# Norms summed on TensorE, three chunks at a layer's start, and weight sums on VectorE in a two-layer float32 encoder

## The chip, the cores and the metric

The kernel runs on one core of a Trainium2 chip. The metric is device time in microseconds (us), from the start of the program to its end, with the host left out. Engines are called PE (TensorE), DVE (VectorE), ACT (ScalarE), POOL (GpSimd) and SP (the queue that issues most transfers).

## The reference

Two batches of 512 tokens (b = 0 and b = 1), width 1024, go through two layers with shared weights, all in float32:

```python
def trunk(x, ...):
    for i in range(2):
        h = rms_norm(x, norm_mix[i])               # x * rsqrt(mean(x*x) + 1e-6) * g
        x = x + (pool_mixer(h, ...) if i == 0 else attention_mixer(h, ...))
        h = rms_norm(x, norm_ffn[i])
        x = x + swiglu_ffn(h, w_gate_up[i], w_down[i])

def swiglu_ffn(h, w_gate_up, w_down):
    gu = h @ w_gate_up                             # 1024 -> 2 x 2816
    g, u = gu[..., :2816], gu[..., 2816:]
    return (silu(g) * u) @ w_down                  # 2816 -> 1024
```

The pool mixer takes centred window means over 2, 4, 8 and 16 tokens minus the token, and multiplies each quarter of the width by a 256 x 256 matrix. The attention has 8 query heads and 2 key heads of 128, with a norm and a rotation on queries and keys.

## The kernel before

**Layout.** x lies transposed: features on partitions, x[:, c, token] with 8 feature chunks c of 128, tokens 0 to 511 for b = 0 and 512 to 1023 for b = 1. A float32 product is made from two fp32r parts of each factor (hi, a cast on ACT; lo, a subtraction on DVE), as three matmuls: hi*hi, hi*lo, lo*hi (`three`).

**Gate and up.** The 2816 hidden features are 22 chunks i of 128. Both batches and both halves of the width are combined in a scheme of seven products instead of eight (`gate_up(layer, i, k)`, k = 1 to 7): the moving tiles are B11 and B21 (b = 0), B22, and the combinations T1 to T4 of both batches; the stationary ones are quarters of the weights (A11, A12, A22) and their sums S1 to S4. One product is 12 matmuls of 128x512. This text writes (i, k) for product k of chunk i: (0, 5) is the first that needs T1, so the first that needs the norm of b = 1. k = 5, 6 and 7 need S1, S2, S3, and k = 3 needs S4. The four sums of a chunk are made of its raw weights: by POOL for chunks 0 and 1 of each layer (`block_sums_13`, `block_sums_24`), by DVE for the others (`block_sums`). POOL also makes the 4 tiles of T3 and the 4 of T4 (`t3_full`, `t4_full`). Each weight part is then cast and subtracted into `ring` (`w_split`). PSUM banks 0 to 2 serve even chunks, 3 to 5 odd ones (`g_bank`), and two sets of four tiles hold their results (`act_tiles`, `snap_*`).

**Down.** Seven products again (q = 0 to 6), of 6 blocks each: 42 blocks, of 24 matmuls, or 12 for a product's last. Block k needs weights `wd` (A11 for q = 0, A12 for q = 1, then sums made in `down_sum`) and activations that come back from memory (`load_act`). SP issues both, in program order; after `load_act(k)` for k = 3 and up come two weight loads each. `load_act(k)` waits until block k - 2 is split. `down_sum(0)` stands on DVE behind `block_lo(3)`, and waits for the first two blocks of A21, which share a semaphore.

**Norms.** Three of them (k = 1: before layer 0's gate/up; 2: before attention; 3: before layer 1's gate/up), for each batch: ACT squares 8 chunks (`square`), POOL adds them one after the other (`add_squares`), PE multiplies the sum by a matrix of ones, so that all partitions hold the sum (`mean_square`), ACT takes the root, DVE the reciprocal of 128x512 (`inverse`), and then DVE scales x (`b0_full`, `b1_full`, `norm_full`).

Every engine's order is written out by hand; semaphores tie them, and an instruction that waits holds up all behind it on its engine.

## Time and profile before

| | us |
|---|---|
| three runs | 1827.1, 1822.15, 1824.36 (median 1824.36) |
| the profiled execution | 1823.22 |
| its span | 1821.4 |
| outside its span | 1.8 |

The granted TensorE clock is 0.976 of full speed over the span. The kernel reads 137.23 MB and writes 44.56 MB, 100 GB/s over the span. A timeline row gives the start, the duration, the engine, line and operation, what is written and read, how many instructions the row merges, and in brackets how long the engine was idle before it and what ended that. A matmul's recorded duration has its latency in it: in a dense stretch one starts each 0.227 us, whatever the row says a single one took. A float32 matmul, not fp32r, is recorded as two.

### The profile page before, as it was taken

How to read it: one execution, taken by the hardware profiler on the slowest of the kernel's cores; microseconds unless marked ns; L12 is line 12 of the kernel's file. 1: busy time of each engine (PE TensorE's matmuls, PEld its weight loads, DVE VectorE, ACT ScalarE, POOL GpSimd, SP SyncE). 2: the span in 40 equal slices, each digit the busy share in tenths (PEclk: the TensorE clock that was granted, in tenths of full speed). 3: DMA queues.
4: the chain of work that ended last, by engine and by line, in shares of the span. 5: the costliest groups of instructions: out<-in, count | busy, mean ns of one | idle time of the engine just before them, and what ended most of it. 6: DMA issues, size and time to landing. Idle time of an engine off the chain costs nothing. (4 is left out here: it accounts for less than half of the span.)

```text
span 1821.4 us, 20998 instructions
## 1 busy us (share of the span) xinstructions
PE 1717.3 (94%) x7741; PEld 1409.0 (77%) x7741; DVE 1205.1 (66%) x1620; ACT 760.7 (42%) x1149; POOL 202.0 (11%) x155
## 2 busy tenths in 40 slices
PE   6779999999999999899998999799999999989998
PEld 6657888888877888778776787578888888878887
DVE  5786656666547756756878877876566665557744
ACT  6543333333333335434576554343333333333332
POOL 1430000000000003322124212500000000000000
PEclk9889999999999999999999999899999999999999
DMA  4003423224275332143112112023233232473333
GB/s 170 24 12 121 129 90 113 93 93 133 76 270 197 101 94 90 58 133 103 42 54 63 35 47 81 24 93 116 87 109 117 93 116 87 156 289 116 95 98 120
DMA packets 185786, 188.40 MB, mean 103 GB/s; under 512 B 8355, under 2 KB 138453, under 8 KB 185685
## 3 DMA queue, kind: packets, MB, share of 16 engines
q1 hardware_dynamic: 112884, 150.36, 25.5%
q10 hardware_dynamic: 72800, 36.70, 6.9%
q8 instruction: 62, 1.02, 0.2%
q14 instruction: 40, 0.32, 0.1%
HBM read 137.23 MB, written 44.56 MB: 100 GB/s over the span
## 5 line engine op out<-in xcount | busy, mean ns | idle before, releaser
L664 PE MATMUL bank<-h_T,ring 128*128 128x512 f32 x2112 | 508.9, 393 | 20.0 <-DVE h_T L1512 11.2
L664 PEld LDWEIGHTS bank<-h_T,ring 128*128 128x128 f32 x2112 | 399.8, 190 | 108.6 <-issue 10.8
L689 PE MATMUL bank<-a,w 128*128 128x512 f32 x1848 | 426.1, 393 | 10.9 <-DVE a L1638 10.9
L689 PEld LDWEIGHTS bank<-a,w 128*128 128x128 f32 x1848 | 349.8, 190 | 85.8 <-issue 12.9
L664 PE MATMUL bank<-h_B,ring 128*128 128x512 f32 x1584 | 388.9, 395 | 9.9 <-ACT tmp L1037 4.3
L664 PEld LDWEIGHTS bank<-h_B,ring 128*128 128x128 f32 x1584 | 300.6, 190 | 78.4 <-ACT tmp L1037 5.2
L1565 DVE TENSOR_TENSOR ring<-raw,ring 128x512 fp32r<-128x512 f32 (+1 forms) x178 | 147.7, 831 | 48.3 <-ACT ring L1016 48.1
L1016 ACT CAST ring<-raw 128x512 fp32r<-128x512 f32 (+1 forms) x178 | 128.5, 722 | 69.7 <-PE bank L664 53.7
L1090 ACT CAST w<-wd_A 128x1024 fp32r<-128x1024 f32 x72 | 70.6, 981 | 199.8 <-PE bank L689 199.8
L1634 DVE TENSOR_TENSOR w<-wd_A,w 128x1024 fp32r<-128x1024 f32 x72 | 82.6, 1147 | 97.3 <-ACT w L1090 97.2
L2112 POOL TENSOR_TENSOR tmp<-tmp,tmp 128x512 f32<-128x512 f32 x42 | 62.5, 1488 | 749.8 <-ACT tmp L938 747.5
L546 PE MATMUL bank<-half_hi,aw 128*128 128x512 f32 x320 | 111.9, 408 | 4.6 <-DVE aw L1459 3.9
L1577 DVE TENSOR_TENSOR tmp<-bank,tmp 128x512 f32<-128x512 f32 x44 | 30.4, 691 | 124.9 <-PE bank L664 124.6
L1638 DVE TENSOR_TENSOR a<-raw,a 128x1024 fp32r<-128x1024 f32 x84 | 97.0, 1154 | 6.5 <-ACT a L1092 6.5
L1092 ACT CAST a<-raw 128x1024 fp32r<-128x1024 f32 x84 | 82.0, 977 | 13.1 <-DMA raw<-act_d 13.1
L546 PE MATMUL bank<-o_hi,aw 128*128 128x512 f32 x256 | 85.6, 397 | 1.5 <-DVE x L1979 1.5
L1016 ACT CAST ring<-s_tmp 128x1024 fp32r<-128x1024 f32 (+1 forms) x46 | 46.7, 1015 | 91.2 <-PE bank L664 85.2
L1343 ACT ACTIVATE prob<-bank,nmax,q_inv 128x512 f32<-128x512 f32 x64 | 49.9, 780 | 70.7 <-DVE nmax L1956 70.7
L546 PEld LDWEIGHTS bank<-half_hi,aw 128*128 128x128 f32 x320 | 61.4, 192 | 19.5 <-issue 3.7
L1053 ACT ACTIVATE tmp<-tmp 128x512 f32<-128x512 f32 x44 | 27.8, 631 | 103.0 <-DVE tmp L1583 103.0
L1565 DVE TENSOR_TENSOR ring<-s_tmp,ring 128x1024 fp32r<-128x1024 f32 (+1 forms) x46 | 54.1, 1177 | 20.7 <-ACT ring L1016 20.7
L1459 DVE TENSOR_TENSOR aw<-raw,aw 128x1024 fp32r<-128x1024 f32 x40 | 54.7, 1369 | 16.6 <-ACT aw L925 16.1
(168 smaller groups left out, 2097.9 us busy)
## 6 DMA issues: line engine op xcount, KB each, us to landing
act_d<-tmp SPq DMA_DIRECT2D x154, 256.0 KB, 3.0
raw<-in_ffn_w_gate_up ACTq DMA_DIRECT2D x70, 512.0 KB, 3.9
raw<-act_d SPq DMA_DIRECT2D x70, 512.0 KB, 3.5
wd_A<-in_ffn_w_down SPq DMA_DIRECT2D x40, 512.0 KB, 6.7
raw<-in_attn_w_qkv SPq DMA_DIRECT2D x24, 512.0 KB, 3.9
raw<-in_ffn_w_gate_up SPq DMA_DIRECT2D x18, 512.0 KB, 4.2
raw<-in_attn_w_o SPq DMA_DIRECT2D x16, 512.0 KB, 4.2
tmp<-tmp SPq DMA_DIRECT2D x80, 64.0 KB, 2.0
```

The source lines that it names most:

```text
L546: ins = pe.matmul(out, w, m, start=first and i == 0, stop=last and i == n - 1)
L664: ins = pe.matmul(out[:, :], w, m, start=k in (1, 2, 5) and j == 0 and t == 0, stop=k in (2, 3, 4) and j == 3 and t == 2, skip_group_check ...
L689: ins = pe.matmul(banks[m][:, :], w, h, start=q in (0, 1, 3) and first and t == 0, stop=q in (1, 5, 6) and jj == NBLK - 1 and t == 2, skip ...
L1016: nc.scalar.copy(dst, src).then_inc(f_hi, 1)
L1090: nc.scalar.copy(w2[:, k % 3, 0:n, 0, :], src).then_inc(w2_hi, 1)
L1092: nc.scalar.copy(a2[:, (k + 1) % 3, 0:n, 0, :], raw2[:, act_slot(layer, k), 0:n, :]).then_inc(a2_hi, 1)
L1343: nc.scalar.activation(prob[:, i, :], b_score[s % 2][:, :], ACT.Exp, bias=nmax[:, s % 8:s % 8 + 1], scale=q_inv[:, s:s + 1], accum_out=rsu ...
L1459: nc.vector.tensor_tensor(aw[:, slot(i), 1, :], raw[:, i % RAW, :], aw[:, slot(i), 0, :].bitcast(F32), ALU.subtract).then_inc(w_lo, 1)
L1565: nc.vector.tensor_tensor(lo, src, hi.bitcast(F32), ALU.subtract).then_inc(f_lo, 1)
L1634: nc.vector.tensor_tensor(w2[:, k % 3, 0:n, 1, :], src, w2[:, k % 3, 0:n, 0, :].bitcast(F32), ALU.subtract).then_inc(w2_lo, 1)
L1638: nc.vector.tensor_tensor(a2[:, s, 0:n, 1, :], raw2[:, act_slot(layer, k), 0:n, :], a2[:, s, 0:n, 0, :].bitcast(F32), ALU.subtract).then_i ...
L2112: nc.gpsimd.tensor_tensor(out=stat[b][:, :], in0=stat[b][:, :], in1=sqr[i % 2][:, :], op=ALU.add).then_inc(n_acc, 1)
```

## The change

- **Norms.** PE sums the squares. A tile of squares is the stationary side and a column of ones the moving one, four small matmuls to a tile (`columns`, `sum_square`), added up in one PSUM bank. This gives the sum of each token in a column, so root and reciprocal work on 128x4. DVE multiplies the identity by it (a diagonal), PE multiplies ones by the diagonal, which spreads it over all partitions (`wide`), and ACT copies that to `stat` (`keep_wide`). For k = 1 all 16 tiles are summed so, for k = 2 the last 4, for k = 3 the last; POOL adds up the others as before, and PE takes that sum in by columns too.
- **Start of a layer's gate/up.** Chunk 2 gets banks 6, 7 and 2, so that (1, 1), (1, 2), (2, 1) run ahead of (0, 5). The tiles of results are seven instead of eight: silu of g0 goes where g1's was, and T4 goes into a tile of the even chunk.
- **Weight sums.** DVE makes all block sums, and T3 and T4; POOL none.
- **Down loads.** A12's first two blocks are loaded ahead of the last stores, and A21 and A22 in pairs.

```diff
+        DIRECT = {1: SEQ[1], 2: SEQ[2][12:], 3: SEQ[3][15:]}
-        g_bank = [bank[0:3], bank[3:6]]
+        g_bank = [bank[0:3], bank[3:6], [bank[6], bank[7], bank[2]]]
...
+            def columns(src, out, first):
+                for i in range(NT):
+                    ins = pe.matmul(out[:, i:i + 1], src[:, i * P:(i + 1) * P], ones[:, 0:1],
+                                    start=first and i == 0, stop=True, skip_group_check=True)
+                return ins
+            def wide(k, b, out):
+                pe.wait_ge(n_diag, 2 * (k - 1) + b + 1)
+                pe.matmul(out[:, :], ones[:, :], diag[k][:, :], start=True, stop=True).then_inc(n_wide, 1)
...
             def square(k, r, ready):
+                    if i - ADD0[k] > len(sq_ring[k]):
+                        act.wait_ge(n_add, i - len(sq_ring[k]))
...
             def inverse(k, b):
+                cols = n_inv[:, NT * b:NT * (b + 1)]
                 dve.wait_ge(n_sqrt, 2 * (k - 1) + b + 1)
-                nc.vector.reciprocal(stat[b][:, :], stat[b][:, :]).then_inc(n_rstd, 1)
+                nc.vector.reciprocal(cols, cols).then_inc(n_rstd, 1)
+                nc.vector.tensor_tensor(diag[k][:, :].rearrange("p (i t) -> p i t", i=NT),
+                                        ident[:, :].unsqueeze(1).to_broadcast([P, NT, P]),
+                                        cols.unsqueeze(2).to_broadcast([P, NT, P]), ALU.mult).then_inc(n_diag, 1)
...
+            for c in range(4):
+                sum_square(1, c, bank[3])
+            turn_x(1, range(4))
+            for c in range(4, KC):
+                sum_square(1, c, bank[3])
+            turn_x(1, range(4, KC))
+            wide(1, 0, bank[3])
+            pool(1, 3)
...
             def swiglu(layer):                     # PE
                 gate_up(layer, 0, 1)
-                mean_square(k, 1, bank[7])
+                if layer == 0:
+                    sum_square(1, 14, bank[3])
+                else:
+                    mean_square(3, 1, bank[3])
+                sum_square(k, 15, bank[3])
                 gate_up(layer, 0, 2)
+                wide(k, 1, bank[5])
                 gate_up(layer, 1, 1)
+                gate_up(layer, 1, 2)
+                gate_up(layer, 2, 1)
                 gate_up(layer, 0, 5)
-                gate_up(layer, 1, 2)
+                gate_up(layer, 2, 2)
                 gate_up(layer, 1, 5)
...
                 for b in range(N_BLOCK):
                     if layer == 0 and b == N_BLOCK - NBLK + 2:
-                        mean_square(2, 0, bank[1])
+                        mean_square(2, 0, bank[1]).then_inc(n_ms, 1)
+                    elif layer == 0 and b == N_BLOCK - NBLK + 4:
+                        wide(2, 0, bank[1])
...
-            project(0, b_gate[0], 0)
-            mean_square(2, 1, b_down[3])
-            project(1, b_gate[1], 0)
+            for quarter in range(3):
+                project(0, b_gate[0], 0, quarter)
+            mean_square(2, 1, b_up[1])
+            for r in range(12, 16):
+                sum_square(2, r, b_up[1])
+            project(0, b_gate[0], 0, 3)
+            project(1, b_gate[1], 0, 0)
+            project(1, b_gate[1], 0, 1)
+            wide(2, 1, b_up[1])
+            project(1, b_gate[1], 0, 2)
+            project(1, b_gate[1], 0, 3)
...
              for w in range(7, 16):
                 project_out(w)
-                if w == 9:
-                    mean_square(3, 0, bank[1])
+                if w == 8:
+                    mean_square(3, 0, bank[1]).then_inc(n_ms, 1)
+                elif w == 9:
+                    wide(3, 0, bank[1])
...
+            def t4_full(layer, j):                 # DVE, was POOL's
+            def t3_full(layer, j):
...
                 later = []
-                for jj in range(NBLK):
-                    if jj < 3:
-                        later += [("A12", 2 * jj), ("A12", 2 * jj + 1)]
-                    later += [("A21", jj), ("A22", jj)]
+                for jj in range(0, NBLK, 2):
+                    later += [("A21", jj), ("A21", jj + 1), ("A22", jj), ("A22", jj + 1)]
+                    if jj < 4:
+                        later += [("A12", jj + 2), ("A12", jj + 3)]
```

How the order moves, at three places. First PE, where layer 0's gate/up begins. h0_B11, h0_B21, h0_T1 and h0_T2 are the moving tiles; a row with h0 is one product, and its bank tells the chunk (0 to 2: chunk 0; 3 to 5: chunk 1). Before:

```order
L664 MATMUL bank0<-h0_B11_80,ring_98 128x512 x12
L559 MATMUL bank7<-tmp7_77,ones_121 128x512
L664 MATMUL bank1<-h0_B21_81,ring_98 128x512 x12
L664 MATMUL bank3<-h0_B11_80,ring_98 128x512 x12
L664 MATMUL bank2<-h0_T1_86,ring_98 128x512 x12
L664 MATMUL bank4<-h0_B21_81,ring_98 128x512 x12
L664 MATMUL bank5<-h0_T1_86,ring_98 128x512 x12
L664 MATMUL bank0<-h0_T2_82,ring_98 128x512 x12
```

And now (banks 6 and 7 are chunk 2's):

```order
L725 MATMUL bank0<-h0_B11_80,ring_98 128x512 x12
L577 MATMUL bank3<-ones_121,tmp2_72 128x1 x4
L577 MATMUL bank3<-ones_121,tmp1_71 128x1 x4
L725 MATMUL bank1<-h0_B21_81,ring_98 128x512 x12
L598 MATMUL bank5<-tmp3_73,ones_121 128x512
L725 MATMUL bank3<-h0_B11_80,ring_98 128x512 x12
L725 MATMUL bank4<-h0_B21_81,ring_98 128x512 x12
L725 MATMUL bank6<-h0_B11_80,ring_98 128x512 x12
L725 MATMUL bank2<-h0_T1_86,ring_98 128x512 x12
L725 MATMUL bank7<-h0_B21_81,ring_98 128x512 x12
L725 MATMUL bank5<-h0_T1_86,ring_98 128x512 x12
L725 MATMUL bank0<-h0_T2_82,ring_98 128x512 x12
```

Between the norm's matmul (L559, now L598) and the first product on T1 stands one product before, and three now; one more, (2, 2), stands before (1, 5).

Second PE again, in the last product of layer 0's down, where the norm for the attention is made. A block is eight rows like those with a2 (four for the last). Before, ahead of block 38, then now, at the end of block 39 and the start of block 40:

```order
L689 MATMUL bank5<-a2_107,w2_106 128x512 x3
L559 MATMUL bank1<-tmp6_76,ones_121 128x512
L689 MATMUL bank6<-a2_107,w2_106 128x512 x3
L689 MATMUL bank7<-a2_107,w2_106 128x512 x3
L689 MATMUL bank4<-a2_107,w2_106 128x512 x3
```

```order
L750 MATMUL bank4<-a2_107,w2_106 128x512 x3
L750 MATMUL bank5<-a2_107,w2_106 128x512 x3
L598 MATMUL bank1<-tmp1_71,ones_121 128x512
L750 MATMUL bank6<-a2_107,w2_106 128x512 x3
L750 MATMUL bank7<-a2_107,w2_106 128x512 x3
```

The column sums (L577) stand where L559 stood, and the matmul that spreads the result stands two blocks later.

Third SP, from the last down load of A11 on (raw2 is the tile of `load_act`; the rows that write act_d are stores). Before:

```order
L388 DMA wd_A11_100<-in_ffn_w_down 128x512
L352 DMA act_d<-tmp5_75 128x512
...
L407 DMA raw2_108<-act_d 128x1024
L388 DMA wd_A12_101<-in_ffn_w_down 128x2x512 x2
L407 DMA raw2_108<-act_d 128x1024
L388 DMA wd_A21_102<-in_ffn_w_down 128x2x512
L388 DMA wd_A22_103<-in_ffn_w_down 128x2x512
L407 DMA raw2_108<-act_d 128x512
L388 DMA wd_A12_101<-in_ffn_w_down 128x2x512 x2
L407 DMA raw2_108<-act_d 128x1024
L388 DMA wd_A21_102<-in_ffn_w_down 128x2x512
```

And now:

```order
L405 DMA wd_A11_100<-in_ffn_w_down 128x512
L405 DMA wd_A12_101<-in_ffn_w_down 128x2x512 x2
L369 DMA act_d<-tmp5_75 128x512
...
L424 DMA raw2_108<-act_d 128x1024
L405 DMA wd_A21_102<-in_ffn_w_down 128x2x512 x2
L424 DMA raw2_108<-act_d 128x1024
L405 DMA wd_A22_103<-in_ffn_w_down 128x2x512 x2
L424 DMA raw2_108<-act_d 128x512
L405 DMA wd_A12_101<-in_ffn_w_down 128x2x512 x2
```

The first rows of raw2 in both are `load_act(3)`. The second load of A21 stood behind `load_act(6)`; it stands behind `load_act(3)` now.

## Rows read from the trace of the kernel before

**Rows 1.** Page, part 1: busy us, share of the span, instructions.

```profile
PE 1717.3 (94%) x7741; PEld 1409.0 (77%) x7741; DVE 1205.1 (66%) x1620; ACT 760.7 (42%) x1149; POOL 202.0 (11%) x155
```

**Rows 2.** Waits of PE: total us, times, longest us.

```profile
PE bank L559 <- POOL tmp L2112: 14.0, 4, 8.5
PE bank L689 <- DVE a L1638: 10.9, 4, 4.8
```

**Rows 3.** Timeline of PE, layer 0's first norm, b = 0.

```profile
47.58 2.07 PE L559 MATMUL bank<-tmp,ones 128*128 128x512 f32 x2 [3.18 <-POOL tmp L2112]
...
56.50 0.47 PE L546 MATMUL bank<-half_hi,pw_hi 128*128 128x512 f32 x1 [0.48 <-ACT x L1111]
```

**Rows 4.** Timeline of PE, layer 0's gate/up, chunks 0 to 2.

```profile
71.59 2.88 PE L664 MATMUL bank<-h_B,ring 128*128 128x512 f32 x12
...
84.08 7.71 PE L664 MATMUL bank<-h_B,ring 128*128 128x512 f32 x24
...
108.58 4.40 PE L664 MATMUL bank<-h_T,ring 128*128 128x512 f32 x18 [2.11 <-DVE ring L1565]
...
158.22 2.88 PE L664 MATMUL bank<-h_T,ring 128*128 128x512 f32 x12
```

**Rows 5.** Timeline of PE, layer 1's start of gate/up, chunks 0 to 2.

```profile
1116.79 0.47 PE L546 MATMUL bank<-o_hi,aw 128*128 128x512 f32 x1 [1.54 <-DVE x L1979]
...
1144.08 2.88 PE L664 MATMUL bank<-h_B,ring 128*128 128x512 f32 x12
...
1162.53 1.62 PE L664 MATMUL bank<-h_T,ring 128*128 128x512 f32 x3 [5.80 <-DVE h_T L1512]
...
1175.12 6.68 PE L664 MATMUL bank<-h_T,ring 128*128 128x512 f32 x21 [2.84 <-DVE ring L1565]
...
1223.68 2.88 PE L664 MATMUL bank<-h_B,ring 128*128 128x512 f32 x12
1226.40 2.88 PE L664 MATMUL bank<-h_T,ring 128*128 128x512 f32 x12
```

**Rows 6.** Timeline of DVE, the same stretch.

```profile
1153.54 3.35 DVE L1465 RECIPROCAL tmp<-tmp 128x512 f32<-128x512 f32 x1
...
1182.94 5.75 DVE L1531 TENSOR_TENSOR h_B<-f_t,h_B 128x512 fp32r<-128x512 f32 x4
...
1189.22 2.48 DVE L1537 TENSOR_TENSOR h_T<-f_t,h_T 128x512 fp32r<-128x512 f32 x4
```

**Rows 7.** Timeline of PE, layer 0's down and layer 1's, block 4 first in each.

```profile
549.96 50.34 PE L689 MATMUL bank<-a,w 128*128 128x512 f32 x210 [4.62 <-DVE a L1638]
...
1618.90 21.27 PE L689 MATMUL bank<-a,w 128*128 128x512 f32 x83 [4.82 <-DVE a L1638]
```

**Rows 8.** Timeline of DVE, layer 1's down, `down_sum(0)`.

```profile
1615.26 1.22 DVE L1652 TENSOR_TENSOR wd_A<-wd_A,wd_A 128x1024 f32<-128x1024 f32 x1 [10.46 <-DMA wd_A<-in_ffn_w_down]
```

**Rows 9.** Windows of PE: stretch, us, busy (count), granted clock, DMA share, GB/s.

```profile
549.00:552.00 3.00, 2.04 (x5) 0.50 0.35 78
```

**Rows 10.** Timeline of PE around layer 0's end of down.

```profile
721.17 1.11 PE L559 MATMUL bank<-tmp,ones 128*128 128x512 f32 x2
721.71 19.65 PE L689 MATMUL bank<-a,w 128*128 128x512 f32 x84
742.97 0.50 PE L546 MATMUL bank<-half_hi,aw 128*128 128x512 f32 x1 [1.61 <-DVE aw L1459]
```

**Rows 11.** Timeline of DVE, first scaling by the attention's norm, b = 0 and b = 1.

```profile
728.79 1.41 DVE L1474 SCALAR_TENSOR_TENSOR tmp<-x,vec,tmp 128x512 f32<-128x512 f32 x2
...
757.39 1.42 DVE L1474 SCALAR_TENSOR_TENSOR tmp<-x,vec,tmp 128x512 f32<-128x512 f32 x2
```

**Rows 12.** Timeline: a reciprocal of 128x4; then four column matmuls among dense ones.

```profile
12.23 0.18 DVE L1684 RECIPROCAL tok_rms<-tok_rms 128x4 f32<-128x4 f32 x1 [12.23 <-ACT tok_rms L1106]
...
794.17 0.95 PE L781 MATMUL bank<-ones,tmp 128*128 128x1 f32 x8
794.98 0.48 PE L546 MATMUL bank<-half_hi,aw 128*128 128x512 f32 x1
```

More of the change, by code:

```diff
@@ L436, in load_ffn @@
                     load_wd(layer, "A11", jj)
+                for jj in range(2):
+                    load_wd(layer, "A12", jj)
                 store_act1(layer, NF - 1)
@@ L554, in w_chunk, with sum_square, turn_x @@
                 return aw[:, slot(i), 0, k * P:(k + 1) * P], aw[:, slot(i), 1, k * P:(k + 1) * P]
-            def mean_square(k, b, out):
-                pe.wait_ge(n_acc, 14 * (k - 1) + acc_count(k, last_of(k, b)))
-                pe.matmul(out[:, :], ones[:, :], stat[b][:, :], start=True, stop=True).then_inc(n_ms, 1)
-            pe.wait_ge(ident_made, 2)
-            def turn_x(b):
-                for i in range(NT):
-                    pe.wait_ge(x_in[NT * b + i], 16)
-                for c in range(KC):
+            def columns(src, out, first):
[3 more added lines that the diff above has]
+                return ins
+            def sum_square(k, r, out):
+                c, b = SEQ[k][r]
+                pe.wait_ge(n_sq, 16 * (k - 1) + r + 1)
+                if k == 1 and r == KC:
+                    pe.wait_ge(n_stat, 1)
+                ins = columns(sq_tile(k, r), out, k == 1 and c == 0)
+                ins.then_inc(n_add, 1)
+            def mean_square(k, b, out):
+                pe.wait_ge(n_acc, acc_count(k, last_of(k, b)))
+                return columns(stat[b], out, True)
+            def wide(k, b, out):
+                pe.wait_ge(n_diag, 2 * (k - 1) + b + 1)
+                pe.matmul(out[:, :], ones[:, :], diag[k][:, :], start=True, stop=True).then_inc(n_wide, 1)
+            pe.wait_ge(ident_made, 2)
+            def turn_x(b, chunks):
+                if chunks[0] == 0:
+                    for i in range(NT):
+                        pe.wait_ge(x_in[NT * b + i], 16)
+                for c in chunks:
                     q = KC * b + c
@@ L616, in mix @@
                     product(b_down[q % 4][:, :], parts, True, True, m_filled)
[L618 removed]
+            turn_x(0, range(KC))
             pe.wait_ge(band_landed, 16)
[L620 to L634 removed]
+            for c in range(4):
+                pool(0, c)
+            mix(0, 0)
+            pool(0, 4)
+            pool(0, 5)
+            mix(0, 1)
+            pool(0, 6)
+            pool(0, 7)
+            mix(0, 2)
+            mix(0, 3)
+            for c in range(3):
+                pool(1, c)
+            for c in range(4):
+                sum_square(1, c, bank[3])
[5 more added lines that the diff above has]
+            pool(1, 3)
+            mix(1, 0)
+            pool(1, 4)
+            pool(1, 5)
+            mix(1, 1)
+            sum_square(1, 8, bank[3])
+            sum_square(1, 9, bank[3])
+            pool(1, 6)
+            pool(1, 7)
+            mix(1, 2)
+            sum_square(1, 10, bank[3])
+            sum_square(1, 11, bank[3])
+            mix(1, 3)
+            sum_square(1, 12, bank[3])
+            sum_square(1, 13, bank[3])
             def gate_up(layer, i, k):
@@ L1310, in _ @@
                 square(2, r, x_ffn0)
+            root(2, 1, b_up[1])
             gain(0, b_gate[0])
             split_next(0)
-            root(2, 1, b_down[3])
-            for c in range(4):
+            keep_wide(2, 1, b_up[1])
+            for c in range(2):
                 norm_hi(1, c)
@@ L1318, in _ @@
             split_next(1)
-            for c in range(4, KC):
+            for c in range(2, KC):
                 norm_hi(1, c)
@@ L1802, in swiglu @@
                 t2_full(layer, 2)
+                t4_full(layer, 2)
                 t2_lo(layer, 1)
@@ L1805, in swiglu @@
                 t2_full(layer, 3)
+                t4_full(layer, 3)
                 t2_lo(layer, 2)
-                add_c11(layer, 1)
                 t2_lo(layer, 3)
+                add_c11(layer, 2)
                 for j in range(4):
                     b22_lo(layer, j)
+                for j in range(4):
+                    t3_full(layer, j)
                 w_split(layer, 1, G_S2)
@@ L1859, in swiglu @@
                     block_lo(layer, k)
-                    if 3 <= k < 27:
-                        down_sum(layer, k - 3)
+                    if 4 <= k < 28:
+                        down_sum(layer, k - 4)
                     if k > 6 and k % 6 == 1:
@@ L1865, in _ @@
             swiglu(0)
-            for k in range(38, 41):
-                block_lo(0, k)
+            block_lo(0, 38)
+            block_lo(0, 39)
             inverse(2, 0)
+            block_lo(0, 40)
             norm_full(0, 0)
```

382 lines of the change are left out of this document (194 added, 188 removed).

## The prediction

> **What bounds the kernel now.** First the page: PE is busy for 1717.3 us of the span, DVE for 1205.1 [rows 1]. PE is the bound, and only its idle stretches, its slow ones and its added work matter. Then PE's waits: two releasers stand out, POOL's sums of squares, 14.0 us, and DVE's split of activations in the down part, 10.9 us [rows 2]. Then PE's timeline, to find where the rest is lost. A product starts 2.72 us after the one before in a dense stretch (1223.68 to 1226.40) [rows 5]. So the 21 products of chunks 0 to 2 need 57.1 us. Layer 0 takes from 71.59 to 160.94 (158.22 + 2.72) for them, 89.4 us [rows 4]; layer 1 from 1144.08 to 1229.12, 85.0 us [rows 5]. So 32 and 28 us are lost in the two starts, part of it waiting on DVE. DVE's timeline in that stretch shows a reciprocal of 3.35 us, and operations that take 1.44 us beside POOL (5.75 for four) and 0.62 without it (2.48 for four) [rows 6]. Each down part loses one wait, 4.62 and 4.82 us [rows 7], and DVE then sat 10.46 us on a weight load [rows 8]. After such a wait the granted clock is 0.50, the 1.2 GHz level, at 549 to 552 us [rows 9]: PE was idle for 4.62 us before. The 210 matmuls behind it take 50.34 us, where 210 x 0.227 + 0.16 is 47.8: the slow clock costs 2.5 us more [rows 7].
>
> **Prices.** A reciprocal of 128x4 is 0.18 us [rows 12]; with the diagonal's multiplication (a DVE operation of 128x512, 0.62) and a dependence of 0.1, `inverse` falls from 3.35 to 0.9 us. Four column matmuls hold PE for 0.81 (794.17 to 794.98) to 0.95 us [rows 12]; I take 0.9. There are 21 tiles summed so and 4 sums of POOL taken in so: 25 x 0.9 = 22.5 us more for PE, of which only what fell into waits is free. `wide` is the same matmul as the old one, about 1.0 us, 6 of them as before. The Trainium skill (TensorE: Matmul & The Clock Gate, section "Wait — 56ns, not 53.3ns?") lets a matmul with few columns start about 25 ns after the last; by that the eight recorded parts would take 0.2 us, the 25 groups 5 us, and the forecast would be 17 us lower, as an estimate from that page. The rows 12 do not show that: the stationary side has to be loaded each time. I go by the row.
>
> **Layer 0's pool stage and start: -2.5 us.** Before, PE waits 3.18 us for POOL's sum and reaches `mix(1, 0)` at 56.50 [rows 3]. Now at 44.4 (47.58 less the wait) come four column sums (3.6), 16 of 32 transposes, four sums (3.6), 16 transposes: 57.4. (The 32 transposes take 5.8: they and `pool(1, 3)` lie between 49.6 and 56.0 [rows 3].) Root and `inverse` run beside the last of these; `wide` 1.0 and `pool(1, 3)` 0.9 lead to `mix(1, 0)` at 59.3, 2.8 late. From there the old kernel took 15.1 us to (0, 1); now six sums are added, 5.4, and each pair stands behind a square that waits for DVE's addition of the mixer's result, since it is placed right after the product that feeds it: about 1.5, 1.3 and 0.5 us. (0, 1) starts at 82.6, against 71.59. But the old kernel then waited for POOL and started (0, 2) at 84.08, 24 matmuls in 7.71 us for 5.6 [rows 4]; the new one starts it at 87.2, after two more sums. `wide` ends at 90.9. By the walk below, (2, 4) ends 65.4 us later, 156.5, against 160.94: -4.4. I keep -2.5, since small matmuls and waits may leave the clock low in this stage. Bounds: -7 and +5.
>
> **Layer 1's start: -9.5 us.** The walk, by rows 5 and 6. The norm of b = 0 is ready some 2.4 us earlier (its reciprocal is that much shorter), so the wait of 1.54 goes, and 0.9 of column sums comes: (0, 1) at 1143.4. Two sums, (0, 2) after its weights: 1151.3. DVE first makes chunk 0's four sums and splits behind them, then `inverse`; `wide` ends at 1153.1. Then (1, 1), (1, 2), (2, 1), with 0.7 for a split, and (0, 5), (2, 2): 1167.7. The old wait of 5.80 before (0, 5) is gone: T1 is ready at 1162.5, when PE comes to it at 1162.2. Next comes (1, 5), which needs S1 of chunk 1. DVE has 28 operations from `wide` to that split (6 scalings of b = 1, 10 tiles of T1, T2 and T4 made or split with their lo parts, 3 additions and 4 block sums among them); at 0.66 us, the mean of 0.62 and 0.70 for those that depend on the last, 18.6 us: 1171.7. So PE waits 4.1 there; the old start of (1, 5) was 1175.12. The clock falls again, 2.5. 14 products follow, 38.1 us, with waits of 1.5 for S2 of chunk 1 (19 DVE operations against three products), 1.0 for g1 of chunk 1 and 1.5 for that of chunk 2 (nothing stands between (i, 7) and (i, 4) there now), and 1.7 for chunk 2's sums: 1171.8 + 38.1 + 2.5 + 5.7 = 1218.1, against 1229.12: -11.0. 1.5 for one more fall of the clock: -9.5. Bounds -13 and -3. DVE's eight moved block sums and tiles (16 operations to a layer, with the four of chunk 0, 9.9 us at 0.62) are inside this: they are paid by POOL's stretching of others (0.82 an operation) and two short reciprocals.
>
> **Down: -7.2 and -7.3 us.** `down_sum(0)` stands behind one block more, and its load is issued three blocks of activations earlier. DVE was free for block 4 at 1604.8 (1615.26 - 10.46) and needs two operations of 1.22 for it [rows 8]: 1607.2; PE comes to it at 1614.1 (1618.90 - 4.82) [rows 7]. What is late next is the load for block 6, behind two blocks of cover. So 4.62 + 2.5 and 4.82 + 2.5 us go. Bounds: all, or nothing.
>
> **The norm before the attention: +8 us.** Here the change costs. The old matmul at 721.17 led to the first scaling at 728.79 [rows 10, 11]. Now the column sums stand there, and `wide` behind blocks 38 and 39: 721.17 + 0.9 + 2 x 5.44 = 732.95. With 1.0 for itself and 0.7 for ACT's copy, DVE scales at 734.7, 5.9 later. From there to PE's first projection it took 14.2 us (742.97 - 728.79), DVE without a gap; so PE starts at 748.9 and idles 6.6 us where it idled 1.61. For b = 1 the old path from there to the next scaling was 14.4 us (757.39 - 742.97). The new one has three quarters of a projection (24 matmuls in all; 4.1), five sums (4.5), a quarter (1.4), half a projection (2.7), `wide` and copy (1.7), and about 2 for the clock: 16.4, so the scaling comes 8 us late. The waits behind it (DVE's chain into the keys) move with it, while PE comes 10 us late, so some of the old waits shrink. +8, bounds +5 and +12. Dense PE work follows, and nothing gives it back.
>
> **Sum.** -2.5 - 7.2 + 8.0 - 9.5 - 7.3 = -18.5. Against the profiled execution's 1823.22 us this is 1804.7; the median shown is 1.1 above it: 1806.
>
> **Rivals.**
> - *The early work gains nothing (1818 us).* The column matmuls keep PE at 1.2 GHz in both starts and the new gaps add falls. For it: after 4.62 us of idle the clock is 0.50 [rows 9]. Against: the sums before (0, 1) in layer 1 stand in dense work. Layer 0's start is then +7, layer 1's -7: 12 more than forecast.
> - *The attention's norm is free (1798 us).* The +8 would not show if the old chain had slack. Against: PE waited 1.61 on it at 742.97 [rows 10], so there was none.
> - *The down wait only moves (1820 us).* The same bytes queue on the same 16 DMA engines; another load, A12's or block 6's activations, is late instead. For it: the wait of 10.46 us on a transfer of 512 KB [rows 8] shows a queue. Then 14.5 us stay.
> - *DVE pays (slower, 1832 us).* The 32 operations moved to DVE in the two starts go at the 1.44 us of rows 6 and not at 0.62, in the stretch where DVE is what PE waits for: 32 x 0.82 = 26 us. It decides from 0.56 us an operation over 0.62. Against: 1.44 is seen only where POOL runs, and POOL has nothing left there.
>
> **Numbers.** Below, a measurement of this kernel can tell 0.3% from no change, 5.5 us. Chances: the forecast 0.62 (its own range 1799 to 1813), early work gains nothing 0.14, norm free 0.08, down wait moves 0.09, DVE pays 0.07. Faster is below 1818.9: 0.62 + 0.08 + 0.08 of the 0.14 + 0.03 of the 0.09 = 0.81. Slower is above 1829.8: 0.07. The same: 0.12. The range is 1796 to 1820.
>
> **What would show it.** In the new trace: no wait of PE over 1 us at block 4; `wide` of the attention's norm near 733 and PE's gap of 6 to 7 us before the first projection; (0, 1) of layer 0 near 82 and not 72; PE's largest wait in each start before (1, 5), on DVE; RECIPROCAL of 128x512 only for the keys; column sums at 0.9 us. Wrong would be a wait at (0, 5) of several us, DVE operations at 1.4 us in the starts, or the first projection at 743.

## The result, and the profile after

The changed kernel takes 1808.9 us, the median of its first five runs (1807.7 to 1820.1), a ratio of 0.9926 to the kernel before, 95% interval 0.990 to 0.9952. Six more runs on another chip gave 1810.5 us, ratio 0.9928 (0.9901 to 0.9954). The forecast was 1806 us, range 1796 to 1820, with a chance of 0.81 for faster. Faster is what it is, by 14 to 15 us.

Two executions were profiled. The first had a span of 1818.3 us; the second, of the same kernel, 1805.1. Where they part is the lesson of this case, so both are shown. By the granted clock that each of the eleven runs records, they stand for two kinds: the six of 1806.2 to 1808.9 us have 0.984 or 0.985, the three of 1816.3 to 1822.7 us have 0.975 to 0.979, and the two between have 0.982. Waits of PE in the second (total us, times, longest), against [rows 2]:

```profile
PE bank L725 <- DVE ring L1690: 17.3, 9, 4.6
PE bank L564 <- DVE aw L1564: 10.5, 2, 6.6
PE bank L750 <- DVE a L1767: 1.7, 2, 1.3
```

POOL releases PE only once more, for 0.2 us, the down part's wait is 1.7 us in all where it was 10.9 [rows 2], and the two waits of 4.6 and 6.6 us are the ones the prediction named: before (1, 5) and before the attention's first projection.

Timeline of PE, second execution, layer 0 from the norm to chunk 2 (start, us, engine, line, operation, shape, count, idle before and releaser), against [rows 3, 4]:

```profile
43.66 3.63 PE L577 MATMUL bank<-ones,tmp 128*128 128x1 f32 x32
47.15 1.95 PE L619 MATMUL bank<-ident,xin 128*128 128x128 f32 x16
48.93 3.79 PE L577 MATMUL bank<-ones,tmp 128*128 128x1 f32 x32
...
109.21 7.83 PE L725 MATMUL bank<-h_T,ring 128*128 128x512 f32 x24 [4.54 <-DVE ring L1690]
...
153.70 3.06 PE L725 MATMUL bank<-h_T,ring 128*128 128x512 f32 x12 [0.79 <-DVE tmp L1708]
```

The same in the first execution:

```profile
42.41 3.63 PE L577 MATMUL bank<-ones,tmp 128*128 128x1 f32 x32
45.90 2.80 PE L619 MATMUL bank<-ident,xin 128*128 128x128 f32 x16
48.49 6.83 PE L577 MATMUL bank<-ones,tmp 128*128 128x1 f32 x32
...
160.22 3.04 PE L725 MATMUL bank<-h_T,ring 128*128 128x512 f32 x12 [0.78 <-DVE tmp L1708]
```

The four column sums that take 3.79 us in one take 6.83 in the other, with PE idle in neither, and the last row of this start stands at 153.70 or at 160.22. The granted clock tells why: 1.00 is 2.4 GHz, 0.50 is 1.2 GHz. Windows of PE (stretch, us, busy (count), granted clock, DMA share, GB/s), first execution:

```profile
47.00:50.00 3.00, 3.00 (x16) 0.50 0.01 3
50.00:53.00 3.00, 3.00 (x15) 0.50 0.01 3
53.00:56.00 3.00, 3.00 (x15) 0.50 0.00 0
56.00:59.00 3.00, 3.00 (x15) 0.50 0.00 0
...
86.00:89.00 3.00, 3.00 (x9) 0.50 0.00 0
```

Second execution:

```profile
47.00:50.00 3.00, 3.00 (x30) 1.00 0.03 8
50.00:53.00 3.00, 3.00 (x25) 0.88 0.01 3
53.00:56.00 3.00, 3.00 (x17) 0.55 0.00 0
56.00:59.00 3.00, 3.00 (x17) 1.00 0.00 0
```

From 47 to 50 us 16 matmuls start in the first, at 1.2 GHz, and 30 in the second, although PE is recorded busy for the whole of each window. The first has a second fall around 86 us, behind a wait of 1.40 us for a square: there (0, 1), the first product of the gate/up, takes 5.47 us instead of 3.02. Of the 6.5 us between the two ends of this start, the stretch up to `mix(1, 0)` makes 3.7 and that product with its neighbours 2.7.

Around the end of layer 0's down, second execution, against [rows 10]:

```profile
518.93 46.26 PE L750 MATMUL bank<-a,w 128*128 128x512 f32 x203 [0.42 <-DVE a L1767]
...
709.42 1.04 PE L577 MATMUL bank<-ones,tmp 128*128 128x1 f32 x8
...
721.33 1.02 PE L598 MATMUL bank<-tmp,ones 128*128 128x512 f32 x2
...
737.18 0.79 PE L564 MATMUL bank<-half_hi,aw 128*128 128x512 f32 x1 [6.63 <-DVE aw L1564]
743.54 4.52 PE L577 MATMUL bank<-ones,tmp 128*128 128x1 f32 x40
```

The group of down matmuls is cut at the edge of the view, at 565 us. It runs past the place where block 4 used to wait, and dense: 46.26 us is 203 x 0.227 and the last one's own end. The gap before the first projection is 6.63. Layer 1's start and its down, against [rows 5, 7]:

```profile
1172.62 8.52 PE L725 MATMUL bank<-h_T,ring 128*128 128x512 f32 x24 [4.57 <-DVE ring L1690]
...
1216.97 3.02 PE L725 MATMUL bank<-h_T,ring 128*128 128x512 f32 x12 [0.78 <-DVE tmp L1708]
...
1583.06 57.18 PE L750 MATMUL bank<-a,w 128*128 128x512 f32 x251 [1.32 <-DVE a L1767]
```

The norm's matmul at the output projection's step w = 9, in the kernel before, in the second execution and in the first:

```profile
1108.75 1.02 PE L559 MATMUL bank<-tmp,ones 128*128 128x512 f32 x2
...
1108.84 1.02 PE L598 MATMUL bank<-tmp,ones 128*128 128x512 f32 x2
...
1122.85 1.02 PE L598 MATMUL bank<-tmp,ones 128*128 128x512 f32 x2
```

So the terms can be read off as differences of landmarks, places that both kernels have, between the profile before and the ones after (a product ends 2.72 us behind its start). "The middle" is what lies between the mean ahead of block 38 and this step.

| landmark | before | second execution | term | first execution | term |
|---|---|---|---|---|---|
| end of (2, 4), layer 0 | 160.9 | 156.4 | -4.5 | 162.9 | +2.0 |
| mean ahead of block 38 | 721.17 | 709.42 | -7.2 (down) | 715.96 | -7.2 |
| step w = 9 | 1108.75 | 1108.84 | +11.8 (middle) | 1122.85 | +19.3 |
| end of (2, 4), layer 1 | 1229.1 | 1219.7 | -9.5 | 1233.4 | -9.8 |
| span | 1821.4 | 1805.1 | -6.9 (down) | 1818.3 | -7.4 |
| sum | | | -16.3 | | -3.1 |

The two downs and layer 1's start agree within 0.5 us. Layer 0's start and the middle differ by the clock: summed over windows of 5 us, the first execution has 31 us at half clock up to the mean, the second 17, and in the middle 41 against 27. Half of these differences is 6.9 us each, where the landmarks differ by 6.5 and 7.5.

### The profile page after: what moved, and what is told of

It is laid out like the page before. It is cut to its first block, busy times and chain, and to the rows that moved or that the text cites. A ratio compares the mean times of both kernels' runs of the same rounds, so it can differ in the third digit from the quotient of the medians.

```text
span 1818.3 us, 21416 instructions
## 1 busy us (share of the span) xinstructions
PE 1739.5 (96%) x7941; PEld 1437.3 (79%) x7941; DVE 1187.4 (65%) x1660; ACT 761.4 (42%) x1157; POOL 127.5 (7%) x104
## 4 chain that ended last, share of the span: by engine, by line
PE 41%; DVE 4%; issue 2%; ACT 2%; DMA 1%; SPq 0%; DVEq 0%; ACTq 0%
PE bank L725 21%; PE bank L750 12%; PE bank L564 7%; DVE raw_max L2108 1%; ACT pt_hi L1482 1%; PE bank L920 1%; DVE pt_lo L2162 0%; ACT aw L1005 0%; DVE nmax L2114 0%; DMA raw<-act_d 0%; PE bank L772 0%; DVE aw L1564 0%; DVE ring L1690 0%; DVE f_t L1616 0%; DMA raw<-in_ffn_w_gate_up 0%
## 5 line engine op out<-in xcount | busy, mean ns | idle before, releaser
L750 PE MATMUL bank<-a,w 128*128 128x512 f32 x1848 | 421.2, 390 | 1.2 <-DVE a L1767 1.2
L564 PE MATMUL bank<-half_hi,aw 128*128 128x512 f32 x320 | 118.3, 429 | 11.9 <-DVE aw L1564 10.5
L2269 POOL TENSOR_TENSOR tmp<-tmp,tmp 128x512 f32<-128x512 f32 x23 | 35.7, 1552 | 785.6 <-ACT tmp L1025 784.8
L1183 ACT CAST a<-raw 128x1024 fp32r<-128x1024 f32 x84 | 81.8, 974 | 17.7 <-DMA raw<-act_d 17.6
L564 PEld LDWEIGHTS bank<-half_hi,aw 128*128 128x128 f32 x320 | 65.2, 204 | 27.7 <-DVE aw L1564 7.1
L1146 ACT ACTIVATE tmp<-tmp 128x512 f32<-128x512 f32 x44 | 27.8, 632 | 106.1 <-DVE tmp L1708 106.1
L564 PE MATMUL bank<-half_lo,aw 128*128 128x512 f32 x160 | 66.3, 414 | 0.0
```

The lines of the kernel that those rows point to most:

```text
L564: ins = pe.matmul(out, w, m, start=first and i == 0, stop=last and i == n - 1)
L750: ins = pe.matmul(banks[m][:, :], w, h, start=q in (0, 1, 3) and first and t == 0, stop=q in (1, 5, 6) and jj == NBLK - 1 and t == 2, skip ...
L1183: nc.scalar.copy(a2[:, (k + 1) % 3, 0:n, 0, :], raw2[:, act_slot(layer, k), 0:n, :]).then_inc(a2_hi, 1)
L2269: nc.gpsimd.tensor_tensor(out=stat[b][:, :], in0=stat[b][:, :], in1=sqr[i % 2][:, :], op=ALU.add).then_inc(n_acc, 1)
```

## Experiments

All times are medians; ratios are to the kernel before, run beside each. Its medians were 1824.9 us beside the first four experiments (the changed kernel again, down alone, one block earlier, T3 and T4), 1826.5 beside the next four (block 38, S1, sums twice, dense matmuls) and 1824.6 beside the last two. The changed kernel ran only beside the first four, 14.4 us below the kernel before. Across groups this difference is what compares, and not the time alone.

**The changed kernel again.**

> The changed kernel again, unaltered, for a second profiled execution. The first one took 1820.1 us where its other runs took 1807.7 to 1810.9. If its surplus of 11 us was more time of PE at the half clock and no part of the change, the median is 1806 to 1811 again, the layers' down multiplications are each 7 us shorter than before, layer 1's start 8 to 9 us shorter, and the middle (from the end of layer 0's down to the attention's first scores) is 6 to 8 us longer than before and not 14. If the surplus belongs to the change (a wait that comes and goes), the runs spread over 1808 to 1820 again and the middle is 14 us longer. Layer 0's start is read from it too: about 2 us later than before if the column sums let the clock fall each time, 2.5 us earlier if that was chance.

1810.5 us (1806.2 to 1822.7). Its profile is the second execution above. Layer 0's start ends 4.5 us earlier, not 2 later, so it isn't slow every time. The runs spread more than those of before (1821.4 to 1829.4 in 17), so the second theory isn't wholly wrong either: the surplus comes back in some runs, as the clock. From 1806.2 us at 0.985 to 1822.7 at 0.975 are 16.5 us; a mean clock lower by 0.010 over 1805 us is worth 18, as an estimate. The middle's 11.8 us is more than the 6 to 8 expected.

**Down alone.** The kernel before, with

```diff
+                for jj in range(2):
+                    load_wd(layer, "A12", jj)
...
-                for jj in range(NBLK):
-                    if jj < 3:
-                        later += [("A12", 2 * jj), ("A12", 2 * jj + 1)]
-                    later += [("A21", jj), ("A22", jj)]
+                for jj in range(0, NBLK, 2):
+                    later += [("A21", jj), ("A21", jj + 1), ("A22", jj), ("A22", jj + 1)]
+                    if jj < 4:
+                        later += [("A12", jj + 2), ("A12", jj + 3)]
...
-                    if 3 <= k < 27:
-                        down_sum(layer, k - 3)
+                    if 4 <= k < 28:
+                        down_sum(layer, k - 4)
```

> The kernel before, with only the new order of the down weights' loads and the sums of them made one block later. My theory: the wait of 4.6 and 4.8 us before block 4 and the half clock behind it were bound to the late second load of A21; each layer's down is 7.2 to 7.4 us shorter, together 14.5, so 1824.4 - 14.5 = 1810, a ratio of 0.992. Rival: what it gains is given back by another load that is late now (A22 or A12, a wait inside blocks 5 to 20): 1820 to 1824. If it comes out at 1810, all else in the change together is worth about nothing: the two starts' gains pay for the norm before the attention.

1812.9 us (1810.1 to 1814.8), ratio 0.9929 (0.9914 to 0.9944). The wait at block 4 is gone, and its down parts are 7.4 and 6.9 us shorter (layer 0's: 526.62 to 717.14 where it was 523.29 to 721.17, [rows 10]). The kernel before first, then this one:

```profile
523.29 22.04 PE L689 MATMUL bank<-a,w 128*128 128x512 f32 x96 [0.42 <-DVE a L1638]
...
526.62 38.59 PE L691 MATMUL bank<-a,w 128*128 128x512 f32 x169 [0.43 <-DVE a L1640]
...
717.14 1.12 PE L561 MATMUL bank<-tmp,ones 128*128 128x512 f32 x2
```

It is 12.0 us of the change's 14.4. This run has two moves in it, the order of the loads and `down_sum` one block later (the changed kernel has both); they weren't tried apart. Everything else in the change, three chunks at the start, column sums on PE, block sums on DVE, is together worth some 2 us by the medians, and the intervals allow that it is worth nothing. By the traces this isn't because those parts do nothing, but because -14.0 in the two starts stands against +11.8 in the middle.

**The attention's norm one block earlier**, then in the middle of block 38.

```diff
-                    elif layer == 0 and b == N_BLOCK - NBLK + 4:
+                    elif layer == 0 and b == N_BLOCK - NBLK + 3:
                         wide(2, 0, bank[1])
```

> The changed kernel, with the matmul that spreads the attention's norm over 128 rows placed one block of the down multiplication earlier (before block 39, not before block 40; a block is 5.1 us of PE). Everything behind it (copy, scaling, the first projection) hangs on it. My theory: the 6.6 us for which PE waits before the first projection shrinks to 1 to 2 us, the half clock behind it goes, and the kernel is 5 to 8 us faster than the changed one: 1801 to 1804, a ratio to the kernel before of 0.988. Rival: the reciprocal and the diagonal are made only at 718.2, PE then waits ahead of block 39 instead, or DVE is the one that is late (its own blocks are behind the norm): not faster than 1807.

> The changed kernel, with the matmul that spreads the attention's norm placed between the two halves of block 38, some 2.7 us behind the column sums that it depends on and two and a half blocks... one and a half blocks ahead of where the change has it. One block earlier shortened the wait before the first projection from 6.6 to 1.2 us and the kernel from about 1809.5 to 1807.0. My theory: the diagonal is ready 2.3 us behind the column sums (mean columns 1.0, root 0.3, reciprocal 0.2, multiplication 0.7), so PE waits for under 0.5 us there, the wait before the first projection goes to 0, and the kernel is 1 to 2 us faster than with one block: 1805 to 1806. Rival: the scalings now stand ahead of DVE's splits of blocks 39 and 40 and PE waits 1 to 3 us for those instead: 1807 to 1809.

One block earlier: 1807.0 us, ratio 0.9897 (0.9874 to 0.9921). In block 38: 1808.8, 0.9891 (0.9867 to 0.9916), two of its six runs at 1797.0 and 1798.7 with a granted clock of 0.986 and 0.987, four at 1808.5 to 1812.1 with 0.979 to 0.982. Timeline of PE, one block earlier:

```profile
709.40 1.04 PE L577 MATMUL bank<-ones,tmp 128*128 128x1 f32 x8
715.84 1.02 PE L598 MATMUL bank<-tmp,ones 128*128 128x512 f32 x2
731.71 0.50 PE L564 MATMUL bank<-half_hi,aw 128*128 128x512 f32 x1 [1.21 <-DVE aw L1564]
735.92 6.32 PE L577 MATMUL bank<-ones,tmp 128*128 128x1 f32 x40
```

The first projection comes 22.3 us behind the mean instead of 27.8, so 5.4 of the term's 5.9 us was this one placement. In block 38 no wait stands before the projection at all: the diagonal is ready 2.3 us behind the column sums, as expected, and the rival (PE waits for blocks 39 and 40 instead) didn't show. But the medians are 17.9 and 17.7 us below the kernel before, where the changed kernel's is 14.4: a gain of 3.5 and 3.3, where 5 to 8, and 1 to 2 more for block 38, were expected. One block earlier, 4.8 us of the 5.4 are still there at the first transposes of the softmax (147.0 us behind the mean for 151.9). From there to w = 9 the same instructions take 251.3 us for 247.6, with 14 us at half clock for 10, so the gain shrinks to 1.1 in this profile. The five column sums run in part at half clock too, 6.32 for 4.52. With a spread of 14 to 15 us, the two placements aren't told apart.

**T3 and T4 back on GpSimd.**

```diff
-                t4_full(layer, 0)
-                t4_full(layer, 1)
...
+            def swiglu(layer):
+                for j in range(4):
+                    ... nc.gpsimd.tensor_tensor(out=f_t4[:, j, 1, :], ... op=ALU.subtract)
+                for j in range(4):
+                    ... nc.gpsimd.tensor_tensor(out=f_t3[:, j, 1, :], ... op=ALU.subtract)
```

> The changed kernel, with the eight differences that make T3 and T4 given back to GpSimd in each layer, as the kernel before had them; the rest is as changed. Theory one (GpSimd's work stretches what VectorE does beside it, 1.4 us in place of 0.6 to 0.75 for an operation): the start of each layer is 2 to 6 us longer, 1812 to 1818. Theory two (VectorE is what PE waits for there, and every operation taken off it is a gain; eight of 0.62 us are 5 us): each start is 1 to 4 us shorter, 1802 to 1807. Neither: within 1 us, since PE waits for the first splits of chunk 1 and those are ahead of it.

1820.3 us in 12 runs (1815.6 to 1825.5), ratio 0.997 (0.9957 to 0.9984): 9.7 us slower than the changed kernel, with eight operations fewer on DVE in each layer. Timeline of DVE, this kernel:

```profile
112.42 1.64 DVE L1632 TENSOR_TENSOR f_t<-f_t,f_t 128x512 f32<-128x512 f32 x1
...
124.82 5.16 DVE L1646 TENSOR_TENSOR h_B<-f_t,h_B 128x512 fp32r<-128x512 f32 x4
```

The changed kernel, second execution, the same four splits, and four differences that GpSimd had:

```profile
115.61 2.49 DVE L1655 TENSOR_TENSOR h_B<-f_t,h_B 128x512 fp32r<-128x512 f32 x4
118.02 2.49 DVE L1649 TENSOR_TENSOR f_t<-f_t 128x512 f32<-128x512 f32 x4
```

Without GpSimd DVE splits four tiles and makes four more in 4.9 us (115.61 to 120.5); with it, the four splits alone take 5.16. Each start is 3 us longer by the landmarks, if layer 0's is held against the first execution of the changed kernel, which has the same long fall of the clock. The other 4 us go with the clock: the four runs here at 0.982 took 1815.9 to 1817.0 us, the changed kernel's two at 0.982 took 1810.9 and 1812.7, and the median run here has 0.981 where that of the changed kernel lies between 0.982 and 0.984. Whether GpSimd's work makes the clock fall more often wasn't tried.

**S1 of chunk 1 earlier.**

```diff
                 block_sums(layer, 1)
+                w_split(layer, 1, G_S1)
...
                 t2_lo(layer, 0)
-                w_split(layer, 1, G_S1)
```

> The changed kernel, with ScalarE's and VectorE's split of S1 of chunk 1 placed directly behind the block sums that make it, ahead of six operations per half for T2 and T4; in each layer. PE's longest wait in each start, 4.6 us before product (1, 5), is on this split, and the clock is at half for some 3 us behind it. My theory: about 10 VectorE operations of 0.61 us stand between the sums and the split, so (1, 5) starts 4 us earlier and its fall of the clock goes, but T2's lo parts come 0.6 us later each; half of the gain is taken back by the wait before (0, 6): 2 to 5 us per layer, 1800 to 1806. Rival: VectorE is the bound of the whole stretch, whatever its order, so PE only waits later (before (0, 6) or (0, 3)) and the kernel is within 1 us of the changed one, 1809.

1810.6 us, ratio 0.9924: the rival. The wait of 4.6 us before (1, 5) is gone, and three waits for T2's lo parts stand before (0, 6):

```profile
109.08 0.93 PE L725 MATMUL bank<-h_T,ring 128*128 128x512 f32 x3 [1.83 <-DVE h_T L1640]
...
114.42 2.92 PE L725 MATMUL bank<-h_T,ring 128*128 128x512 f32 x6 [1.07 <-DVE h_T L1640]
...
153.47 3.06 PE L725 MATMUL bank<-h_T,ring 128*128 128x512 f32 x12 [0.79 <-DVE tmp L1708]
```

The last product of the stretch starts at 153.47 for 153.70. By this run what bounds it is how much DVE does, and not in which order, at least for this one operation moved. It fits with this that POOL's stretching mattered.

**Column sums twice.**

```diff
+                if k == 1:
+                    columns(sq_tile(k, r), out[:, 8:16], c == 0)
                 ins = columns(sq_tile(k, r), out, k == 1 and c == 0)
```

> The changed kernel, with each of the first norm's 16 column sums made twice (the second copy into columns that nobody reads). This measures the price of a column sum on PE's path: 16 x 0.9 = 14 us if each holds PE for what its row says and the clock falls are as before (1823 to 1825), 16 x 0.2 = 3 us if matmuls with one column follow each other in 25 ns (1812), and more than 14, to 1830, if the longer sparse stretch makes the clock fall in every execution.

1841.8 us, ratio 1.0093 (1.0078 to 1.0108), all four runs within 5.1 us: 15.3 above the kernel before where the changed one is 14.4 below, so some 30 us more for 16 column sums. By the profile the start ends at 186.3 us for 156.4, the same 30.

```profile
42.65 9.51 PE L577 MATMUL bank<-ones,tmp 128*128 128x1 f32 x64
...
55.47 13.65 PE L577 MATMUL bank<-ones,tmp 128*128 128x1 f32 x64
...
83.39 3.73 PE L577 MATMUL bank<-ones,tmp 128*128 128x1 f32 x32 [0.59 <-ACT tmp L1027]
```

In the mixer's stage, at full clock, two sums made twice take 3.73 us for 1.95 (the changed kernel's 65.80), so 0.89 us a sum: the price in the prediction holds. In the long blocks four of them take up to 6.8 us: there the half clock costs as much again as the instructions (16 x 0.89 is 14 of the 30). The clock stays at 0.50 from 50 to 74 us here.

**Dense matmuls between.** Two matmuls of 128x256 ahead of each of the eight sums. The kernel then lacks the right sums for the first norm of b = 0, and serves for its time alone; the other work and the waits are the same.

```diff
+                if k == 1 and b == 0:
+                    for _ in range(2):
+                        pe.matmul(out[:, 256:512], pw_hi[:, 0, 0:P], pw_hi[:, 0, 0:256], ...)
                 ins = columns(sq_tile(k, r), out, k == 1 and c == 0)
```

> The changed kernel, with two extra matmuls of 128x256 (both sides of the mixer's high parts, into unused columns of the same bank; nothing reads them) ahead of each of the eight column sums of the first norm, b = 0. It adds about 16 x 0.12 = 2 us of PE work. In two executions of the changed kernel the same column sums ran once with the clock at half from 47 to 60 us, and once with full clock until 52.5; the end of layer 0's start was 6.5 us apart. Theory one (the sparse column matmuls make the throttle see too little work): with dense ones between them the clock holds through the sums in each execution, the second four take 3.8 and not 6.8 us, runs above 1812 become rare: 1808 to 1810. Theory two (the fall comes by itself, or from the transposes): the extra work costs its 2 us and the falls stay, 1811 to 1813.

1813.8 us, ratio 0.9942 (0.9929 to 0.9955), five of six runs within 2.1 us, one 5 above. It is 12.6 us below the kernel before, so some 2 us are lost: theory two by the median. The sums themselves stayed at 0.95 us each but one, yet the clock fell in the transposes around them:

```profile
47.00:50.00 3.00, 3.00 (x20) 0.65 0.01 3
50.00:53.00 3.00, 3.00 (x23) 0.78 0.01 3
...
56.00:59.00 3.00, 3.00 (x15) 0.50 0.00 0
```

The fall is shorter than in the first execution, but the start ends at 164.0 us, later than there (162.9): here the added work cost what it gained. So the next try was order and not filler.

**Sums in pairs.** Lines that follow each other are joined by semicolons here and below.

```diff
             mix(0, 2)
-            mix(0, 3)
+            sum_square(1, 0, bank[3]); sum_square(1, 1, bank[3])
             for c in range(3):
                 pool(1, c)
-            for c in range(4):
-                sum_square(1, c, bank[3])
-            turn_x(1, range(4))
-            for c in range(4, KC):
-                sum_square(1, c, bank[3])
-            turn_x(1, range(4, KC))
+            sum_square(1, 2, bank[3]); sum_square(1, 3, bank[3])
+            mix(0, 3)
+            sum_square(1, 4, bank[3]); sum_square(1, 5, bank[3])
+            turn_x(1, range(2))
+            sum_square(1, 6, bank[3]); sum_square(1, 7, bank[3])
+            turn_x(1, range(2, KC))
```

> The changed kernel, with the eight column sums of the first norm, b = 0, no longer in two blocks of four (32 sparse matmuls each) but in pairs: two behind mix(0, 2), two behind the three pools of b = 1, two behind mix(0, 3), and two behind the first two groups of transposes. The same instructions, only PE's order. Made twice, these sums cost 32 us where 16 groups of 0.9 account for 14, the rest was the clock; and in the changed kernel the stretch from 43 us on ran either at half clock for 13 us or for 3 us. Theory one (a long stretch of sparse matmuls is what lets the clock fall): in pairs between dense products the clock holds to the transposes, the start of layer 0 ends at 156 us in every execution and runs above 1812 become rare: median 1805 to 1808. Theory two (the transposes and waits are what it falls in, wherever the sums stand): median 1809 to 1811, spread as before. It could also lose: mix(0, 3) and with it the squares of the last two tiles come 5 us later, so the norm may be late by 2 us.

1810.9 us, ratio 0.993 (0.9913 to 0.9947), 1808.8 to 1815.4. Windows of this kernel:

```profile
50.00:53.00 3.00, 3.00 (x30) 1.00 0.01 3
...
65.00:68.00 3.00, 3.00 (x22) 0.81 0.02 5
68.00:71.00 3.00, 3.00 (x15) 0.62 0.00 0
```

Through the sums and transposes, from 40 to 65 us, the clock now holds at full, and the runs spread over 6.6 us where the changed kernel's spread over 16.5. But the median doesn't move: 13.8 us below the kernel before, for 14.4. Of theory one only the first half is right: the fall comes one stage later, in the two sums and two pools (matmuls of 136 columns) from 65 us on, where the changed kernel's second execution ran at 1.00, and the start ends at 157.3 (154.60 + 2.72) for 156.4. What the pairs took away is the long fall, not the fall.

**Both moves, and the attention's sums between the projection's quarters.** The pairs above and `wide` in block 38, not shown again, and

```diff
-            for quarter in range(3):
-                project(0, b_gate[0], 0, quarter)
-            mean_square(2, 1, b_up[1])
-            for r in range(12, 16):
-                sum_square(2, r, b_up[1])
-            project(0, b_gate[0], 0, 3)
+            project(0, b_gate[0], 0, 0)
+            project(0, b_gate[0], 0, 1)
+            mean_square(2, 1, b_up[1]); sum_square(2, 12, b_up[1])
+            project(0, b_gate[0], 0, 2)
+            sum_square(2, 13, b_up[1]); sum_square(2, 14, b_up[1])
+            project(0, b_gate[0], 0, 3)
+            sum_square(2, 15, b_up[1])
```

> spread, with two more moves: the matmul that spreads the attention's norm, b = 0, in the middle of block 38 (this alone gave 1797 to 1812 in six runs, a wait of 6.6 us gone), and the five column sums of its b = 1 no longer in a row behind three quarters of the first projection (6.2 us at half clock in two profiles, 4.5 at full) but one to two between its quarters. If the sparse stretches make the clock fall and the moves add up: 1796 to 1801, a ratio of 0.986. If the falls only move: 1804 to 1808, no better than with the one move.

1799.7 us (1797.9 to 1800.0 in four runs), ratio 0.9861 (0.9841 to 0.988): faster than both kernels, and with the narrowest spread. Timeline of PE, the kernel before last:

```profile
710.20 1.04 PE L577 MATMUL bank<-ones,tmp 128*128 128x1 f32 x8
713.91 1.02 PE L598 MATMUL bank<-tmp,ones 128*128 128x512 f32 x2
...
850.93 1.82 PE L927 MATMUL bank<-ident,prob 128*128 128x128 f32 x12 [2.13 <-DVE prob L2128]
...
861.90 2.33 PE L842 MATMUL bank<-ident,prob 128*128 128x128 f32 x12 [2.13 <-DVE prob L1963]
```

From the mean to the first transposes of the softmax it takes 140.7 us (850.93 - 710.20), the changed kernel 151.9, the kernel before 140.7 as well (721.17 to 861.90). All that the change lost up to there is back. The five column sums of b = 1, in three groups now, take 4.63 us together, at full clock. From the softmax to w = 9 it takes 251.2 us, where the kernel before takes 246.9, so of the middle's 11.8 us 7.5 are back in this profile. The four runs have a granted clock of 0.986 to 0.989, and they are no faster than the two fast runs of block 38 alone (1797.0 and 1798.7 at 0.986 and 0.987): what the added moves seem to buy is that the good case comes each time, four in four instead of two in six. Which of them does it wasn't tried apart, and these are few runs.

## Why the prediction was right

The time and the sign were right. Each term by its own landmark:

- *Down, -7.2 and -7.3.* Measured -7.2 and -6.9; alone, -7.4 and -6.9 by the landmarks and 12 us in the medians. The arithmetic (a wait of 4.7 and 2.5 of slow clock behind it) was complete, and no wait for another load took its place: that rival is out.
- *Layer 1's start, -9.5.* Measured -9.5 and -9.8. The wait before (1, 5) was worked out as 4.1 and is 4.57; DVE's operations there take 0.6 to 0.7 us. DVE pays, the slower rival, failed as reasoned: with GpSimd idle nothing is stretched, and giving it back eight operations brings operations of 1.7 us back.
- *Layer 0's start, -2.5.* The walk gave -4.4 and I set it back by 1.9 for the clock. It is -4.5 where the clock falls for 3 us among the sums and +2.0 where it falls for 13 there and again at 86 us. That the walk meets the first is luck in part: `wide` ends at 89.1 us and not at 90.9, and (2, 4) ends 67.3 us behind it and not 65.4, two errors of some 2 us that cancel. (The walk's own additions slip by up to 0.5 us too: its parts give 83.1 for (0, 1), not 82.6, and 65.0 us for the stretch behind `wide`, not 65.4.) The rival "early work gains nothing" describes the other. It isn't one number but two, and the execution decides. The rival had +7 for this stage and a chance of 0.14; some of it happens, in some runs, for this stage and not for layer 1's, and the middle, which the rival left out, loses as much to the clock.
- *The norm before the attention, +8.* The first projection is 5.96 us later (5.9 forecast) with 6.63 idle before it (6.6). The path for b = 1, from the first projection to the next scaling, was set at 16.4 us and takes 19.1 (737.18 to 756.26): the three quarters take 6.4 us and not 4.1, behind a wait that had been priced at "about 2 for the clock" for the whole path, and a head's matmul of 1.0 between the quarters was left out. Another 1 lies behind it and wasn't traced further. The term is +11.8, just within its bounds, 3.8 more than stated; in the first execution it is +19.3, far outside them, with the clock on top.

So what held the sum near was an error of 2.0 one way and 3.8 the other, which is luck: -16.3 for -18.5 by the second profile. The first, at 1820.1 us, lies at the very edge of the range. The forecast took the clock as a fixed price in each stage; the runs show it as the largest difference between two executions of one kernel. The comparison by medians gives -14.4 and -15.5.

The rule of the Trainium skill that was weighed (TensorE: Matmul & The Clock Gate, section "Wait — 56ns, not 53.3ns?") would have made the sums nearly free. The doubled sums decide: 0.89 us for each, not the 0.2 estimated from that page.

What stays open: in which stretches the changed kernel's slowest runs (1816.3 and 1822.7 us, at a clock of 0.979 and 0.975) lose their time, since only two executions were profiled, and what makes the clock fall in one execution and hold in the next, with the same instructions.

## What to carry over

When a change has several parts, run the cheapest part alone: here a new order of loads, with its sums one block later, was 12 us of 14.4, and the large rewrite paid for itself only after its one bad placement was mended. A producer's result should be picked up as soon as it is ready, by its own time (2.3 us here) and not by whole blocks of the consumer's loop. And matmuls of one column in a long row can cost their time twice, in some executions. In pairs between dense products they lost the long fall here, though the pairs by themselves didn't move the median. When runs of one kernel spread, read the granted clock of each before looking for a wait.

## What the runs showed of the hardware

- PE without an idle moment isn't PE at full clock. Among column matmuls and 128x128 transposes the granted clock went to 0.50, the 1.2 GHz level, for some 13 us in one execution and 3 us in another of the same kernel, and the times of its eleven runs follow their granted clock, 1806.2 us at 0.985 to 1822.7 at 0.975.
- DVE operations of 128x512 take 0.6 to 0.7 us with GpSimd idle, and mostly 1.3 to 1.8 us when they start beside a GpSimd tensor operation (1.7 us itself). Moving eight operations a layer off DVE lost 9.7 us in the medians, some 6 of it in the two starts.
- A group of four fp32 column matmuls, recorded as eight, holds PE for 0.89 us at full clock and about 1.7 at half (6.83 for four groups), although one column is streamed. The weight loads of these matmuls follow each other without a gap (busy for 3.20 of 3.20 us from 43.8 to 47.0); that they set the price is argued from this and wasn't tried alone.
